# Eleven gate projections moved from the first attention into the levels of the delta net

## The reference, cut to what matters

```python
mod = silu(c) @ w_ada + b_ada                  # 6 x 1024: shifts, scales, gates of the block
sh1, sc1, gt1, sh2, sc2, gt2 = split(mod, 6)   # the last four are needed after the delta net
h = rmsnorm(x) * (1 + sc1) + sh1               # (the same for the context, with its own modulation)
p = h @ w_in                                   # 39 tiles of 128 columns: q, k, v, delta-net q, k, v,
q_a, k_a, v_a, qkv_d, z_d, a, b, gates = split(p)      # z, decays; the last 16 tiles are gates
g_attn, g_dn = split(sigmoid(gates + b_gate), 2)       # needed when the branches are merged
o_attn = windowed_attention(q_a, k_a, v_a, context keys and values, sink)
# gated delta rule, forwards and backwards; per chunk:
#   t_inv = inverse of (I + A), A strictly triangular, by products that double the block size
#   W, U = t_inv @ keys, t_inv @ values
#   v_new = U - W @ S;  o = q @ S + attn @ v_new;  S = S * decay + k.T @ v_new
o_dn = bidirectional_delta(...)
x = x + gt1 * ((g_attn * (o_attn @ w_br_attn) + g_dn * (o_dn @ w_br_dn)) @ w_out)
# then a product-key expert layer, and the whole second block
```

## Time and profile before

| | us |
|---|---|
| median of 3 runs (lowest, highest) | 1781.78 (1777.49, 1782.66) |
| the profiled execution | 1772.43 |
| its span, first to last instruction | 1770.6 |
| PE busy / chain of waits on PE | 1700.2 (96%) / 80% |
| DVE busy | 1308.8 (74%) |
| ACT busy | 1057.5 (60%) |
| POOL busy | 161.3 (9%) |
| mean granted clock of PE | 0.989 |
| one 512 KB load, issue to landing, median of 525 | 3.3 |

### The profile page before, as it was taken

One profiled execution on the slowest core, in us unless ns is written; L12 is line 12 of the kernel. 1 busy time (PEld: TensorE's weight loads), 2 busy tenths in 40 slices (PEclk: granted clock), 3 DMA queues, 4 the chain that ended last, 5 costly groups with the idle time before them and its releaser, 6 DMA issues.

```text
span 1770.6 us, 34144 instructions
## 1 busy us (share of the span) xinstructions
PE 1700.2 (96%) x11488; PEld 1513.5 (85%) x11488; DVE 1308.8 (74%) x2648; ACT 1057.5 (60%) x2182; POOL 161.3 (9%) x136
## 2 busy tenths in 40 slices
PE   7999997899999999999999999999899999999998
PEld 1877776689999978888899999999799899999997
DVE  3787677767989799667766666666776768878887
ACT  2545454445665699666555555555557666666666
POOL 0000003411548200000000000000010000010000
PEclk9999999999999999999999999999999999999999
DMA  8534441215455511455555555555364544555553
GB/s 303 186 99 140 156 154 60 84 47 199 161 178 178 166 37 48 166 191 196 193 185 185 189 189 184 186 188 189 119 209 142 176 141 133 177 184 185 187 181 129
DMA packets 77272, 283.31 MB, mean 160 GB/s; under 512 B 8576, under 2 KB 8576, under 8 KB 76928
## 3 DMA queue, kind: packets, MB, share of 16 engines
q1 hardware_dynamic: 77184, 282.16, 47.6%
HBM read 281.08 MB, written 1.05 MB: 159 GB/s over the span
## 4 chain that ended last, share of the span: by engine, by line
PE 80%; DVE 12%; ACT 4%; issue 2%; POOL 1%; DMA 1%; PEld 0%; PEldq 0%; ACTq 0%; POOLq 0%; DVEq 0%; SPq 0%
PE banks L921 20%; PE banks L909 17%; PE banks L1000 10%; PE banks L497 8%; PE banks L1156 7%; PE banks L1180 3%; PE banks L851 2%; DVE split L2444 2%; DVE arena L2440 2%; PE banks L465 1%; PE banks L1014 1%; PE banks L1116 1%; PE banks L821 1%; PE banks L541 1%; POOL split L2967 1%
## 5 line engine op out<-in xcount | busy, mean ns | idle before, releaser
L1529 ACT ACTIVATE split<-arena 128x512 fp32r<-128x512 f32 x492 | 308.9, 629 | 134.9 <-PE banks L909 76.8
L909 PEld LDWEIGHTS banks<-split 128*128 128x128 f32 x2880 | 355.4, 192 | 10.5 <-DVE split L2370 3.1
L921 PE MATMUL banks<-split 128*128 128x512 f32 x1536 | 361.9, 390 | 1.0 <-issue 1.0
L909 PE MATMUL banks<-split 128*128 128x256 f32 x2880 | 358.7, 283 | 3.2 <-DVE split L2370 2.3
L2462 DVE TENSOR_TENSOR split<-arena,split 128x512 fp32r<-128x512 f32 x396 | 270.6, 690 | 105.3 <-ACT split L1529 99.5
L921 PEld LDWEIGHTS banks<-split 128*128 128x128 f32 x1536 | 283.8, 188 | 57.3 <-issue 1.4
L1507 ACT ACTIVATE split<-arena 128x512 fp32r<-128x512 f32 x312 | 194.5, 627 | 112.3 <-PE banks L1156 52.9
L1000 PE MATMUL banks<-split 128*128 128x256 f32 x1728 | 216.8, 287 | 4.3 <-DVE split L2540 3.9
L1000 PEld LDWEIGHTS banks<-split 128*128 128x128 f32 x1728 | 211.9, 194 | 7.2 <-issue 6.0
L2517 DVE TENSOR_TENSOR split<-arena,split 128x512 fp32r<-128x512 f32 x180 | 123.7, 698 | 65.6 <-ACT split L1507 64.1
L497 PEld LDWEIGHTS banks<-split 128*128 128x128 f32 (+1 forms) x936 | 134.0, 194 | 28.5 <-issue 13.8
(11 more groups left out here) (421 smaller groups left out, 2311.5 us busy)
## 6 DMA issues: line engine op xcount, KB each, us to landing
arena<-wstream SPq DMA_DIRECT2D x525, 512.0 KB, 3.3
arena<-x_t SPq DMA_DIRECT2D x1, 2048.0 KB, 12.2
arena<-matsa SPq DMA_DIRECT2D x1, 1234.0 KB, 6.3
out_t<-arena SPq DMA_DIRECT2D x4, 256.0 KB, 2.0
arena<-mats SPq DMA_DIRECT2D x1, 576.0 KB, 8.1
arena<-crow SPq DMA_DIRECT2D x1, 512.0 KB, 7.1
arena<-rows SPq DMA_DIRECT2D x1, 512.0 KB, 3.9
arena<-mats SPq DMA_DIRECT2D x1, 449.0 KB, 4.3
```

The lines of the kernel that those rows point to most:

```text
L909: mm = pe.matmul(ps[:, 4 + b, 0:S], w_parts[:, c, (2 * m + half) % 4, P * k:P * k + P], h_parts[:, e, 4 * half + k, :], start=(half == 0 a ...
L921: mm = pe.matmul(ps[:, 2 * tt + half, :], g_parts[:, e, j % 2, P * tt:P * tt + P], w_parts[:, c, (2 * m + half) % 4, :], start=(first and ...
L1529: act.activation(w_parts[:, 0, (2 * m + half) % 4, :], ring[:, peer_slot(m), 512 * half:512 * half + 512], ACT.Copy).then_inc(sem["w_hi"], 1)
```

## The change

- **Stream.** An explicit ORDER of in-tiles and modulation tiles. Modulation tiles are now of two kinds: 12 "pool" tiles, multiplied by POOL and summed by ACT (two instructions, sum_tail waits for the product), and 20 "dve" tiles, made by DVE as before. Eight pool tiles stand behind in-tiles 10 to 17, three dve tiles each behind 25 to 28, the rest behind 29 to 38. SP waits for tail_sum (ACT) before it reuses a pool tile's slot. The row crow is loaded earlier, and its silu stands in in_out(8).
- **Attention.** in_tile(23), (24), (25) stand in groups 0 to 2 and in_tile(26) behind the last; three dve tiles a group on DVE. The roots' products are placed anew.
- **Delta net.** in_tile(27) takes the place of in_tile(38) in the setup; DVE makes the halves of tiles 28 and 29 there. Tiles 28 to 38 are computed in bank 7, half a tile (12 products) in each of the first 22 levels, between the side work and the updates (fill_before), with ACT's fill_out and fill_hi and DVE's in_lo in the levels. Bank 7 is free for this since the scan products share bank 6, one direction after the other: direction 0 in one level, direction 1 in the next; only those of scan step 3 keep 6 + d. U goes into bank 2d, so level 1 of the next chunk waits for both copies (wu_ready). Token turns come one to a level.
- **Modulation in the levels**: one pool tile per chunk (POOL behind its token scalings, ACT at l = 3) and two dve tiles (l = 4 and 6) instead of 14 dve tiles.
- **End**: the sigmoid of gates 8 to 15 and the sqrt of gain3 stand behind the last copies of chunk 3.

```diff
+FIRST_FILL, N_FILL = 28, 11
+TAILS_BEHIND = {**{t: [("pool", t - 10)] for t in range(10, 18)}, **{t: [("dve", 3 * (t - 25) + q) for q in range(3)] for t in range(25, 29)},
+                **{29 + 3 * n: [("pool", 8 + n)] for n in range(4)}, **{30 + 3 * n: [("dve", 12 + 2 * n)] for n in range(3)},
+                **{31 + 3 * n: [("dve", 13 + 2 * n)] for n in range(3)}}
+TAILS_BEHIND[38] += [("dve", 18), ("dve", 19)]
+ORDER = [x for t in range(39) for x in [("in", t)] + TAILS_BEHIND.get(t, [])]
...
+        scan_bank = lambda st, d: 6 if st < 3 else 6 + d
...
             def load_freed_by_splits(lo, hi):
                 for n in range(lo, hi):
+                    kind, q = ORDER[n - RING - N_WIN]
+                    if kind == "in":
+                        sp.wait_ge(sem["in_lo"], 2 * q + 2)
+                    elif kind == "pool":
+                        sp.wait_ge(sem["tail_sum"], q + 1)
                     else:
-                        sp.wait_ge(sem["tail_done"], early_tails[n - RING] + 1)
+                        sp.wait_ge(sem["tail_done"], q + 1)
                     sp.dma_start(tile_at(n), wstream[n]).then_inc(loaded[n % RING], 16)
...
+            def fill_quarter(t, q):
+                if q == 0:
+                    pe.wait_ge(sem["proj_free"], 4 + t)
+                    if t == FIRST_FILL:
+                        pe.wait_ge(sem["a_raw"], 2)
+                if q % 2 == 0:
+                    pe.wait_ge(sem["in_lo"], 2 * t + q // 2 + 1)
+                for k in (2 * q, 2 * q + 1):
+                    for c, e in PASSES:
+                        mm = pe.matmul(ps[:, 7, 0:S], w_parts[:, c, (2 * t + k // 4) % 4, P * (k % 4):P * (k % 4) + P], hp[:, e, k, 0:S], ...)
...
+            def fill_before(step):
+                if step // 2 < N_FILL:
+                    for q in range(2):
+                        fill_quarter(FIRST_FILL + step // 2, 2 * (step % 2) + q)
...
             for g in range(4):
-                a = 23 + 4 * g
                 if g == 1:
                     scores(2)
-                in_tile(a, {2: (spread_roots, 2)} if g == 3 else {})
+                turn_probs(4 * g)
+                turn_probs(4 * g + 1)
+                if g < 3:
+                    in_tile(23 + g, {5: (sum_squares_l2, 0)} if g == 1 else {})
+                else:
+                    spread_roots(0)
...
             def level_products(n, l, d):
-                        pe.wait_ge(sem["w_moved"], step_at(n - 1, d))
+                        pe.wait_ge(sem["wu_ready"], step_at(n - 1, d))
...
+                    if n == 1 and l < 3:
+                        state_write(0, l - 1)
+                    if n >= 2 and l < 3:
+                        state_read(n - 1, l - 1)
+                    if n >= 2 and 3 <= l < 5:
+                        state_write(n - 1, l - 3)
+                    if n == 3 and l >= 5:
+                        out_write(2, l - 5)
...
+                    fill_before(step)
                     for d in range(2):
                         level_update(n, l, d)
...
             def in_out(t):                                     # ACT
...
+                if t == 8:
+                    act.wait_ge(sem["params_in"], 48)
+                    act.activation(crow, crow, ACT.Silu)
                 if 8 <= t < 20:
                     conv_silu(t - 8)
+                if 10 <= t < 18:
+                    sum_tail(t - 10)
+            def sum_tail(q):
+                tile = tile_at(AT["pool", q])
+                act.wait_ge(sem["tail_mult"], q + 1)
+                act.activation(tile, tile, ACT.Copy, accum_out=modT[:, 16 + modulation_of["pool"](q), 0:1]).then_inc(sem["tail_sum"], 1)
...
+                    if step % 2 and step < 2 * N_FILL:         # ACT, in each level
+                        fill_out(FIRST_FILL + step // 2)
+                    if 2 <= step < 2 * N_FILL - 2:
+                        fill_hi(step + 2)
...
+                    if l == 3:
+                        sum_tail(8 + n)
...
+                    i = 6 * n + l                              # DVE, in each level
+                    if 4 <= i < 2 * N_FILL:
+                        in_lo(FIRST_FILL + i // 2, i % 2)
+                    if l in (4, 6):
+                        mod_tail(12 + 2 * n + l // 6)
...
+            def mod_tail(q):                                   # POOL
+                n = AT["pool", q]
+                pool.wait_ge(loaded[n % RING], 16 * (n // RING + 1))
+                pool.tensor_tensor(tile_at(n), tile_at(n), crow, ALU.mult).then_inc(sem["tail_mult"], 1)
+            pool.wait_ge(sem["conv_used"], 1)
+            for q in range(8):
+                mod_tail(q)
```

More of the change, by code:

```diff
@@ L1313, in _ @@
                 in_out(t)
-            act.wait_ge(sem["late_in"], 48)
-            act.activation(crow, crow, ACT.Silu)
+            act.wait_ge(sem["late_in"], 32)
             for t in range(20, 22):
@@ L1391, in _ @@
             tok_move(1)
-            in_out(38)
+            in_out(27)
             tok_move(2)
@@ L1426, in _ @@
                 for l in range(1, 7):
+                    step = 6 * n + l - 1
                     for d in range(2):
@@ L2094, in _ @@
                     link(dve.reciprocal(dec["beta"], dec["beta"]))
-                    l2_scale(3)
-                lo_and_tail(a + 3)
+                    for c in range(3):
+                        l2_scale(c)
                 dve.wait_ge(sem["weighted"], 4 * g + 4)
@@ L2179, in _ @@
             link(dve.tensor_copy(masks[:, :, 0:P], blocks))
-            tails = iter(range(EARLY_TAILS, 32))
-            for q in range(2):
-                mod_tail(next(tails))
+            both_lo(28)
             link(dve.tensor_tensor(gain3[:, 0, :], col("final_norm"), col("final_norm"), ALU.mult))
```

251 lines of the change are left out of this document (123 added, 128 removed).

## The result

The changed kernel took 1817.2 us in the median of four runs (1813.8 to 1818.0), the kernel before 1781.4 on the same chip: a ratio of 1.020, with a 95% interval of 1.018 to 1.022. The direction was as forecast, the size was not: 1791 was forecast, with 1804 as the upper end, and the rival that came nearest (D, 1812) had the low clock in the wrong stage.

What follows compares the result with a forecast made beforehand. PE's work was taken to bound attention, a PE-DVE chain with holes the levels. Terms 17 - 34.5 - 1 + 27 + 1 = +9.5 us on the profiled 1772.43 gave 1782, plus 9.35 to the medians' scale: 1791 us, range 1776 to 1804.

Steps and rivals of the forecast that it cites:

- D: Projection: PE, idle a third of each step, gets the low clock there; +21 us, 1812 us; chance 0.07.
- the price of attention's last head group: Attention, group 3: six spreads, output turns and 5 us of waits, together 19.4 us.
- Rival C: Projection: loads land before ACT is back, so the ring's new wait is not exposed; +5 at most, 1779 us; chance 0.08.
- the exposed loads: Projection, tiles 13 to 19: ACT waits about 4.5 us for each load; seven steps of 7.8 us instead of 5.44.
- B: Attention: bound by its chain of engines once tiles are gone, only -24 us; sum +20, 1802 us; chance 0.13.
- Rival A: Levels: their holes take the halves, so levels only +8.5 us; sum -9, 1773 us, faster; chance 0.20.
- Projection, +17: Projection: slots released late expose loads on ACT; POOL products and ACT's work cost nothing; +17 us, bounds +12 and +22.
- Attention, -34.5: Attention: eleven tiles leave, PE stays the bound; groups take 57.7 us instead of 90.2; -34.5 us, bounds -36 and -24.
- Setup, -1: Delta net's setup: DVE loses two products (2.4 us), gains halves of tiles 28 and 29; -1 us, range -2 to +1.
- Levels, +27: Delta net's levels: 22 halves of 1.5 us come, mostly paid; 28 less one for clock; +27 us, bounds +34.5 and +8.5.
- End, +1: Kernel's end: second sigmoid and sqrt with table load stand after the last copies; +1 us, range 0 to +3.
- the three l = 6 halves: Levels, l = 6: DVE's first_inverse (4 us) precedes the answer to the update, so these halves cost nothing.

Runs made afterwards that it cites:

- the release mended: Changed kernel with the projection's eight pool-tile sums one step earlier in ScalarE's queue, ahead of the move of the tile's result: 1806.7 us.
- the tile in the gap: Changed kernel with gate tile 26 moved into the fourth head group: 1806.4 us; with spread products over 128 rows as well: 1798.1 us.

## Why the prediction was wrong, step by step

The step that failed is the price of attention's last head group: 19.4 us, at full clock. It took 34.3 us, 27.5 of them at half the clock, and that is most of the miss.

- **Bound and direction: right.** PE's work bounds attention, the levels are a chain with holes, and a tile moved from one to the other is mostly paid. Rival C fell by the exposed loads. B had attention gain too little, as it did, but by a chain of waits, while PE was busy for 80.75 of its 88.99 us. Rival A fell: to be faster, a half had to cost less than 0.85 us, and at +30.6 for 22 of them it costs 1.4.
- **The scale.** The terms were added to 1772.4, the profiled execution, and 9.35 us on top brought the sum to the scale of the medians. The terms add up to +9.5 and the two spans differ by 45.7, so they miss by 36; the forecast of 1791 misses by 26 only, since the changed kernel's profiled execution lies 0.8 us above its median and not 9 below. That part is luck.
- **Projection, +17: mechanism right, 7.5 us short.** Seven exposed loads, as named. Six of them cost ScalarE 4.7 to 6.0 us and the seventh 3.4, in place of 4.5 each, which together makes 2.5. Most of the rest is "the POOL products end a whole step before they are summed; cost nothing": they end in time, but they hold VectorE up. In the changed kernel most fall where VectorE waits for the load anyway and only the first two show (1.8 and 2.1 us in the rows above); with the release mended they cost 12.8 us.
- **Attention, -34.5: the step that failed.** It came to -14.1. The counts were right, and so was the part ahead of the groups (10.3 us, 12.4 before). Group 3 was put at 19.4 us, from durations read among whole tiles at full clock (1.95 for four weighings, 1.12 for a spread pair), in a place from which the change takes those tiles. It took 34.3 us (226.6 to 260.9), 27.5 of them at the low clock. With spread products over 128 rows the stage gives back 9.4 us, with the tile in the gap as well 16 (88.99 to 73.04), and there group 3 takes 17.2 us. The other 6 us stand in groups 0 to 2 (44.3 against 38.3 us), and no run repairs them; group 1 alone took 23.9 in place of 20.6, some 2 us of it at the low clock behind a wait of 3.08 us. Rival D had such a clock in the projection, where it was 0.97; I looked for it where TensorE waits, not where it works. That D's 1812 lies near the result is chance.
- **Setup, -1: it was +2.2**, all of it the low clock carried in; with the spread products over 128 rows alone it is 12.10, -0.1. (Its own terms, 2.4 less, 1.3 and half of 1.3 more, make -0.5 and not -1.)
- **Levels, +27: it was +30.6**, inside the bounds. But the parts were not what I summed. Products 13.5 and splits 4.5 by leaving them out, GpSimd's products 3.7; the last 8.9, among them clock, lone products and the shared bank, could be parted only roughly. So the near hit of this term is in part luck. That the three l = 6 halves cost nothing is wrong: placed ahead of the update they don't fill the wait behind it (5.5 us before and after), placed behind it they do (5.5 us of waits to 0.4; the levels were 3.1 shorter, of which the pool tiles' return has a part that wasn't tried alone).
- **End, +1: 0.** The sigmoid found room.

## What to carry over

A price read from a trace holds for its neighbours too: before products of few rows are left without whole tiles around them, ask what the clock will do there, and widen them to all rows with zeros where the trace shows it low. Count what an operation moved to GpSimd does to VectorE beside it, even if its own result is in time. Work moved from a busy stage to one with holes gains only what stands in the holes themselves: place it behind the instruction whose answer is awaited, or it is mostly paid. And compare a forecast with a trace on the scale of the trace it was read from: one profiled execution can lie 9 us from its median.

## What the runs showed of the hardware

- Few rows. With six rows in its spread products TensorE was busy for 26.8 of 27.5 us and was granted 1.2 GHz throughout; with 128 rows, 122 of them zero, in the same place it was back at 2.4 GHz in 7 us. A pair costs the same at full clock (1.12 and 1.02 to 1.08 us). The Trainium skill, "TensorE: Matmul & The Clock Gate" (HAM oscillation), tells of the low clock behind waits; the fall behind the wait of 3.53 us agrees. The fall at 234.5 us with tile 26 in group 3, behind a wait of 0.47 us, is not of that kind. Why few rows matter no run shows.
- The shared port. A 128x1024 product of GpSimd takes 2.4 us and puts 1.8 to 2.2 us on VectorE's splits, taps or one-input operations on the arena; VectorE's operation that reads a bank kept its 0.68 us beside it (345.77).
- Less work, longer stage. In one pair of traces the levels with 22 products fewer took 5 us more, at 0.87 instead of 0.92 of the clock; the spread of the runs leaves open how often.
